# Feed-forward inputs on Trainium2: one product of 512 columns for high and low activations, and evacuation in two halves

## What is computed

```
D_MODEL = 1024; SEQ = 256; D_FF = 11 * D_MODEL // 4        # 2816
def _rmsnorm(x, g):
    y = x * lax.rsqrt(jnp.mean(x * x, axis=-1, keepdims=True) + 1e-6)
    return y * g
def _swiglu(h, w_in, w_out):
    a, b = jnp.split(h @ w_in, 2, axis=-1)
    return (jax.nn.silu(a) * b) @ w_out
x = x + 0.5 * _swiglu(_rmsnorm(x, g), w_in, w_out)          # four times
```

## Time and profile before

| | us |
|---|---|
| median of 3 runs (2226.9 to 2237.2) | 2232.5 |
| profiled execution, its own time | 2229.4 |
| its span | 2227.7 |
| TensorE (PE) matmuls busy | 2143.9 |
| weight loads (PEld) busy | 1878.6 |
| VectorE (DVE) busy | 1384.0 |
| ScalarE (ACT) busy | 847.6 |

### The profile page before, as it was taken

One profiled execution on the slowest core, in us unless ns is written; L12 is line 12 of the kernel. 1 busy time (PEld: TensorE's weight loads), 2 busy tenths in 40 slices (PEclk: granted clock), 3 DMA queues, 4 the chain that ended last, 5 costly groups with the idle time before them and its releaser, 6 DMA issues.

```text
span 2227.7 us, 43246 instructions
## 1 busy us (share of the span) xinstructions
PE 2143.9 (96%) x17274; PEld 1878.6 (84%) x17274; DVE 1384.0 (62%) x2303; ACT 847.6 (38%) x1336; POOL 28.9 (1%) x58
## 2 busy tenths in 40 slices
PE   7999999999999999899999999999999999999998
PEld 7999878999999998899986676788888876559987
DVE  6666657666666677766664556674355355657854
ACT  4444634444444444444531444421111233334332
POOL 0000000000000000000000000000000000000000
PEclk9999999999999999999999999999999999989999
DMA  7665424665666552466641110222222222003544
GB/s 269 245 228 185 167 75 175 241 238 183 240 237 224 198 182 99 167 229 246 226 176 38 39 39 20 102 76 94 94 95 94 95 95 95 1 19 120 182 174 147
DMA packets 50229, 325.73 MB, mean 146 GB/s; under 512 B 5328, under 2 KB 8656, under 8 KB 16976
## 3 DMA queue, kind: packets, MB, share of 16 engines
q1 hardware_dynamic: 42480, 266.62, 33.7%
q0 software_dynamic: 7648, 57.71, 6.9%
HBM read 323.26 MB, written 1.05 MB: 146 GB/s over the span
## 4 chain that ended last, share of the span: by engine, by line
PE 84%; DVE 9%; ACT 4%; issue 2%; DMA 0%; ACTq 0%; DVEq 0%; SPq 0%
PE psum L1914 17%; PE psum L1915 16%; PE psum L1916 16%; PE psum L2002 4%; PE psum L2003 4%; PE psum L2004 4%; PE psum L2499 3%; DVE w_lo L1062 2%; PE psum L2023 2%; PE psum L2338 2%; PE psum L2500 1%; ACT scratch L866 1%; ACT w_hi L620 1%; PE psum L2358 1%; PE psum L2321 1%
## 5 line engine op out<-in xcount | busy, mean ns | idle before, releaser
L1062 DVE TENSOR_TENSOR w_lo<-raw,w_hi 128x1024 fp32r<-128x1024 f32 (+1 forms) x534 | 590.2, 1146 | 229.3 <-ACT w_hi L620 215.3
L620 ACT ACTIVATE w_hi<-raw 128x1024 fp32r<-128x1024 f32 (+1 forms) x542 | 514.6, 991 | 572.3 <-PE psum L1916 351.6
L1914 PE MATMUL psum<-h_hi,w_hi 128*128 128x256 f32 (+1 forms) x2136 | 641.6, 300 | 12.8 <-DVE w_lo L1062 6.4
L1915 PE MATMUL psum<-h_lo,w_hi 128*128 128x256 f32 (+1 forms) x2136 | 633.5, 297 | 0.0
L1916 PE MATMUL psum<-h_hi,w_lo 128*128 128x256 f32 (+1 forms) x2136 | 633.1, 296 | 0.0
L1914 PEld LDWEIGHTS psum<-h_hi,w_hi 128*128 128x128 f32 x2136 | 410.1, 192 | 32.7 <-issue 12.8
L1916 PEld LDWEIGHTS psum<-h_hi,w_lo 128*128 128x128 f32 x2136 | 410.5, 192 | 10.1
L1915 PEld LDWEIGHTS psum<-h_lo,w_hi 128*128 128x128 f32 x2136 | 410.5, 192 | 9.8
L2002 PE MATMUL psum<-g_both,w_hi 128*128 128x256 f32 x704 | 202.2, 287 | 3.6 <-DVE w_lo L1062 3.6
L2003 PE MATMUL psum<-g_both,w_hi 128*128 128x256 f32 x704 | 199.3, 283 | 0.0
L2004 PE MATMUL psum<-g_both,w_lo 128*128 128x256 f32 x704 | 199.3, 283 | 0.0
(11 more groups left out here) (349 smaller groups left out, 3250.1 us busy)
## 6 DMA issues: line engine op xcount, KB each, us to landing
raw<-in_weights SPq DMA_DIRECT2D x207, 1024.0 KB, 4.8
raw_ada<-in_ada POOLq DMA_DIRECT2D x48, 1024.0 KB, 6.9
raw<-in_weights SPq DMA_DIRECT2D x64, 704.0 KB, 4.1
arena<-in_rpb POOLq DMA_DIRECT2D x1, 2048.0 KB, 10.9
arena<-in_fox_c POOLq DMA_DIRECT2D x1, 1696.0 KB, 9.2
const_region<-in_latent_c POOLq DMA_DIRECT2D x1, 1394.0 KB, 6.8
const_region<-in_even_c POOLq DMA_DIRECT2D x1, 1360.0 KB, 8.1
x_res<-in_x_lat SPq DMA_DIRECT2D x4, 256.0 KB, 7.1
```

The lines of the kernel that those rows point to most:

```text
L620: nc.scalar.activation(wh[s][:, a], raw[s][:, a], ACT.Copy).then_inc(hi_ready, 1)
L1062: V.tensor_tensor(wl[s][:, a], raw[s][:, a], wh[s][:, a].bitcast(F32), ALU.subtract).then_inc(lo_ready, 1)
L1914: mm(out, sh, mh, start=n == 0, stop=False)
L1915: mm(out, sh, ml, start=False, stop=False)
```

## The change

The activations' high and low parts become one tensor `h_both`. In the feed-forward input (TensorE, `wide_chunks` and `first_wide`), the two matmuls with `w_hi` become one of 512 columns over both parts, whose result takes a whole bank: columns 0 to 255 hold w_hi x high, 256 to 511 w_hi x low. The matmul with `w_lo` adds into columns 0 to 255. The gate half goes to bank 0 or 1 (3 in the first unit) and is signalled by its own semaphore `gate_done`; the value half goes to bank 4 or 5, signalled by `gemm_done`. To get a value, the two parts of a bank have to be added: ScalarE copies columns 256 to 511 to SBUF and VectorE adds them to columns 0 to 255. This happens for the gate half in the unit's own turn, and for the value half in the next turn, behind the conversion of the next panel; the bank is freed by the value half's sum.

```diff
-        hh = sb("h_hi", [P, DC, TJ], F32R)
-        hl = sb("h_lo", [P, DC, TJ], F32R)
+        h_both = sb("h_both", [P, 2, DC, TJ], F32R)
+        hh, hl = h_both[:, 0, :, :], h_both[:, 1, :, :]
...
             def swiglu(i, j):
...
+                if not first:
+                    up_copy(pos.e + 2 * i + j, 1 - j)
+                act.wait_ge(gate_done, n + 1)
+                nc.scalar.activation(ffn_gl, psum[:, FFN_FIRST if first else (pos.u + j) % 2, T:TJ],
+                                     ACT.Copy).then_inc(gate_low, 1)
+                if not first:
+                    g_high(n - 1, 2 * i + j - 1, 1 - j)
                 act.wait_ge(scaled_a, n + 1)
                 nc.scalar.activation(ffn_t[:, j, :], ffn_a[:, j, :], ACT.Tanh, scale=0.5).then_inc(tanh_done, 1)
-                act.wait_ge(bank_free, pos.u + 2 * i + j + 3)
-                nc.scalar.activation(flat(gh, (2 * i + j) * T, T), ffn_g[:, j, :], ACT.Copy).then_inc(g_hi_done, 1)
+
+            def up_copy(e, j, b=None):
+
+                act.wait_ge(gemm_done, e)
+                nc.scalar.activation(ffn_ul, psum[:, UP + ((pos.u + j) % 2 if b is None else b), T:TJ],
+                                     ACT.Copy).then_inc(up_low, 1)
+
+            def g_high(n, c, j):
+
+                act.wait_ge(ffn_made, n + 1)
+                nc.scalar.activation(flat(gh, c * T, T), ffn_g[:, j, :], ACT.Copy).then_inc(g_hi_done, 1)
...
                 stage(11, 2, 1, 2, swiglu, peel=1, lead=lead)
+                up_copy(pos.e, 1, (pos.u - 1) % 2)
+                g_high(pos.n("unit") + 21, 21, 1)
...
+                def up(n, j, u):
+
+                    dve.wait_ge(up_low, n + 1)
+                    V.tensor_tensor(e_tmp[:], psum[:, UP + u % 2, 0:T] if isinstance(u, int) else
+                                    psum[:, UP + (pos.u + j) % 2, 0:T], ffn_ul, ALU.add).then_inc(bank_free, 1)
+                    freed(u)
+                    dve.wait_ge(ffn_seq, n + 1)
+                    V.tensor_tensor(ffn_g[:, j, :], ffn_u[:], e_tmp[:], ALU.mult).then_inc(ffn_made, 1)
...
-                    dve.wait_ge(gemm_done, pos.e + 2 * i + j + 1)
-                    V.tensor_tensor(ffn_a[:, j, :], ps_a, n_inv, ALU.mult).then_inc(scaled_a, 1)
-                    if not (peeled and j == 0):
+                    else:
+                        up(n - 1, 1 - j, u - 1)
+                    dve.wait_ge(gate_low, n + 1)
+                    V.tensor_tensor(n_add, psum[:, FFN_FIRST if first else b, 0:T], ffn_gl, ALU.add).then_inc(gate_sum, 1)
+                    dve.wait_ge(gate_sum, n + 1)
+                    V.tensor_tensor(ffn_a[:, j, :], n_add, n_inv, ALU.mult).then_inc(scaled_a, 1)
+                    if not first:
                         low(n - 1, 1 - j, c - 1)
-                        freed(u - 1)
                     dve.wait_ge(tanh_done, n + 1)
...
-                    V.tensor_tensor(ffn_g[:, j, :], ffn_u[:], ps_b, ALU.mult).then_inc(bank_free, 1)
...
+            def wide_chunks(b, s):
+
+                for m, (o, done) in enumerate(((b, gate_done), (UP + b, gemm_done))):
+                    for k in range(DC):
+                        w_hi, w_lo = wtile(s, k, m, 2 * P)
+                        mm(psum[:, o, :], w_hi, h_both[:, :, k, 0:T], start=k == 0, stop=False)
+                        ins = mm(psum[:, o, 0:T], w_lo, hh[:, k, 0:T], start=False, stop=k == DC - 1)
+                    ins.then_inc(done, 1)
```

More of the change, by code:

```diff
@@ L240, in build @@
         ada_done = sem("ada_done")
+        gate_done, gate_low, gate_sum = sem("gate_done"), sem("gate_low"), sem("gate_sum")
+        up_low, ffn_made = sem("up_low"), sem("ffn_made")
         v_made, v_scaled = sem("v_made"), sem("v_scaled")
@@ L1109, in evac @@
                 def evac(i, j):
                     peeled = isinstance(i, int) and i == 0
+                    first = peeled and j == 0
                     u = pos.u + 2 * i + j
                     n, c = n0 + 2 * i + j, 2 * i + j
-                    bank = (pos.u + j) % 2
-                    ps_a, ps_b = psum[:, bank, 0:T], psum[:, bank, T:2 * T]
-                    if peeled and j == 0:
+                    b = (pos.u + j) % 2
+                    if first:
                         inverse_norm()
-                        ps_a, ps_b = psum[:, FIRST, 0:T], psum[:, FIRST + 1, 0:T]
@@ L1121, in evac @@
+                    V.tensor_tensor(ffn_a[:, j, :], n_add, n_inv, ALU.mult).then_inc(scaled_a, 1)
+                    if not first:
                         low(n - 1, 1 - j, c - 1)
-                        freed(u - 1)
                     dve.wait_ge(tanh_done, n + 1)
+                    if not first:
+                        dve.wait_ge(ffn_made, n)
                     V.scalar_tensor_tensor(ffn_u[:], ffn_t[:, j, :], 1.0, ffn_a[:, j, :], ALU.add,
                                            ALU.mult).then_inc(ffn_seq, 1)
-                    dve.wait_ge(ffn_seq, n + 1)
@@ L1134, in evac, with last @@
                         ada_add(ab + i)
-                return evac, lambda: low(n0 + 21, 1, 21)
+                def last():
+                    up(n0 + 21, 1, pos.u - 1)
+                    low(n0 + 21, 1, 21)
+                return evac, last
             def ada_turn(k):
@@ L1962, in first_chunks, with first_wide @@
                 return ins
+            def wide_chunks(b, s):
[5 more added lines that the diff above has]
+                    ins.then_inc(done, 1)
+            def first_wide(s):
+                for k in range(DC):
+                    if k == DC - 1:
+                        first_sum()
+                    pe.wait_ge(h_ready, pos.n("h", 1))
+                    for m, (o, done) in enumerate(((FFN_FIRST, gate_done), (UP + pos.u % 2, gemm_done))):
+                        w_hi, w_lo = wtile(s, k, m, 2 * P)
+                        mm(psum[:, o, :], w_hi, h_both[:, :, k, 0:T], start=k == 0, stop=False)
+                        ins = mm(psum[:, o, 0:T], w_lo, hh[:, k, 0:T], start=False, stop=k == DC - 1)
+                        if k == DC - 1:
+                            ins.then_inc(done, 1)
             def first_sum():
@@ L1981, in into @@
                     bank(pos.u + 2 * i + j)
[L1982 to L1983 removed]
+                    if isinstance(i, int) and i == 0 and j == 0:
+                        first_wide(s)
+                    else:
+                        wide_chunks((pos.u + j) % 2, s)
                     if j == 0:
```

9 lines of the change are left out of this document (4 added, 5 removed).

## The result

| | before | after |
|---|---|---|
| median, us | 2236.8 (10 runs, 2226.9 to 2239.6) | 2221.4 (10 runs, 2216.3 to 2230.0) |
| profiled execution, own time | 2229.4 | 2225.0 |
| its span | 2227.7 | 2223.3 |
| its granted clock, mean | 0.986 | 0.983 |

The ratio is 0.9936, with an interval of 0.9919 to 0.9953: faster, by 15.5 us between the medians, where 20.9 were forecast. The direction was right and the time lies inside the range, but the largest term of the forecast's sum, the price of a pair of products, came out at half its size. The kernel before has ten runs here and had three when the forecast was made; its median moved from 2232.5 to 2236.8 us, so 4.3 of the 9.8 us between forecast and measured time are no fault of the sum.

A forecast was written before the change was run, and what follows sets the result against it. TensorE's matmul stream in the feed-forward input was taken as the bound. Shorter pairs 17.1, starts 2.0 and ends 1.8 summed to 20.9 us, taken from 2232.5 to forecast 2211.6 us, range 2204 to 2222.

The forecast's parts named there:

- the price of a pair of products: Feed-forward input, TensorE: a group costs 0.3467 us in place of 0.36, worth 17.1 us over 1280 groups.
- What bounds the kernel: Feed-forward input: TensorE is busy 120 of 120 us, so only a shorter TensorE stream helps if other engines keep up.
- Neither bound of the range: Best case 2205.8 us with all edge stalls gone; worst 2219.5 with dearer sums and half a microsecond lost per edge.
- The prediction's own sign of being wrong: Input stage: a turn above 12.4 us, late TensorE stalls on value sum or low part, or pair spacing near 0.36.
- Rival 1: Input stage: separate blocks or switching output forms keep spacing at 0.36 us; only edges pay, 3.8 us, 2228.7; 6 in 100.
- The loop, 5.5 us: VectorE and ScalarE, conversion start to tanh end: 5.5 us against TensorE's 6.16 a unit, so it fits.
- Rival 2: Input units: the loop of VectorE and ScalarE becomes the bound at 6.6 us a unit, 2252 us in all; 4 in 100.
- The added waits at zero: Input units: the bank is free 3.8 us behind a unit's end, TensorE asks at 5.55 or 6.76; no wait added.
- "as before": Turns with a modulation panel: VectorE's transpose waits until about 1.1 us behind the unit's end, unchanged by the change.
- The starts, 0.5 us each: Start of each feed-forward: third unit 7.0 us behind the reciprocal in place of 7.49, 2.0 us over four.
- The ends, 0.45 us each: End of each feed-forward's input: conversion 0.45 us earlier in a stall of 0.94, 1.8 us over four.
- The sum: Whole kernel: 17.1 + 2.0 + 1.8 = 20.9 us gained, giving 2211.6 us.

The follow-up runs named there:

- the run with adjacent blocks: The changed kernel with high and low activations laid side by side chunk by chunk, blocks 2 KB apart in place of 16 KB: 2224.2 us, ratio 0.9962.
- the grouped kernel: The changed kernel with each half of a steady unit running its eight 512-column products first, then its eight of 256: 2217.1 us, ratio 0.9928.

## Why the prediction was wrong, and where it was right

- **What bounds the kernel: right.** TensorE stays busy throughout the window at clock 1.00, and only its stream counts.
- **"The trace holds that pair already ... 0.3467 us each ... 1280 groups x 0.0133 = 17.1 us": this step failed.** The pair does run at 0.3467, in the earlier trace rows and in some stretches after, but steady input turns run at 0.3533. What is saved is 0.36 - 0.3533 = 0.0067 us a group, 8.5 us, or by turns (12.74 - 12.53) x 40 = 8.4. One stretch of 256 pairs in one execution was taken as the price of the form. It was one of two prices, and another run has that very stretch at 0.3537. The gain was the difference of two near numbers, so that 2% more in one of them halved it. Neither bound of the range carried that; that the time lies in it, by 0.6 us, is luck: the room had been left for the edges, which came out near their forecast. The prediction's own sign of being wrong, a turn above 12.4 us, did come: 12.53. The Trainium skill, "TensorE: Matmul & The Clock Gate", "Back-to-back issue gap", gives the formula that the prediction quotes for an isolated matmul and not for a stream; its estimate of 325.0 ns lies further below this price than below the 0.3467.
- **Rival 1, the spacing stays at 0.36: half right.** Half of the saving came. Its first reason, two separate blocks, falls by the run with adjacent blocks. The second, switching between two output forms, has the grouped kernel for it, whose turns are all shorter; against it stand the stretches that alternate at 0.3467, as fast as if switching cost nothing. It stays open.
- **The loop, 5.5 us: right**, at 5.48. The assumed 0.45 for ScalarE's PSUM copy was 0.36 to 0.39. Rival 2 did not come, and the kernel with the value half in its own turn shows what it would have cost.
- **The added waits at zero: right.** No unit behind the third is stalled; the group of L2006 has 2.2 us of waiting for the value sum in all, 3 times. VectorE's transpose waited in the turns with a modulation panel, 39 times and 33.0 us in all; "as before" was wrong, since before it waited 3 times, 5.7 us. It cost TensorE nothing.
- **The starts, 0.5 us each: nearly.** The third unit starts 374.80 - 367.95 = 6.85 us behind the reciprocal, where 7.0 was forecast and 7.49 was before, and in three of the four the value sum releases it, as written. From the second unit's first product it is 0.60 to 0.65 us each, 2.5 in all, for a forecast of 2.0.
- **The ends, 0.45 us each: nearly.** The stall fell from 0.94 to 0.30 in the first; over the four the stretch from the first output product to the second panel's is 2.4 us shorter, for a forecast of 1.8.
- **The sum** with the measured price is 8.5 + 2.5 + 2.4 = 13.4 us, against 13.7 by the trace's stages (8.8 where 8.5 stands). The 15.5 between the medians is that and 1.8 more; the interval of the ratio reaches from 10 to 18 us and can't tell the two apart. 13.4 in place of 20.9 would have put the forecast at 2219.1.

## What to carry to other kernels

Where a gain is the small difference of two spacings, read the spacing in every stretch and every execution that holds the form, and let the range span them: a price from one stretch may be a state. Group products by width where the order is free, rather than alternating two widths; here that took another 0.12 us off each turn, in the one execution that was profiled. When a step's output comes in two parts, signal the first early and put the second's evacuation behind the next conversion, and look at the end of the stage for what the early signal earns: 7 us here, all of it there.

## What the runs showed of the hardware

A stream that alternates products of 512 and 256 columns, each with its own weight load, has two spacings at granted clock 1.00: 0.3467 and 0.3533 us a pair. It holds one for a stretch, up to 255 distances. In the faster (changed kernel, from 29.6 us) the next start comes 0.230 us behind a wide product and 0.117 behind a narrow one. In the slower (same trace, from 36.4 us) the distances repeat after three pairs: 0.240 and 0.120, 0.236 and 0.114, 0.232 and 0.118. So the difference sits behind the wide product.

The stride of the weights, the distance of the blocks, the order of banks and the activations' address don't select the spacing; with a stop or a spare product between stretches other stretches got the faster one. Long streams of one width settle at one spacing, 0.12 us at 256 columns and 0.2267 at 512, in every profiled execution, and their sum is the faster pair. A stream of 512 columns takes a few products to get there: in the kernel before, from 1455.6 us, after a first distance of 0.307 they are 0.235, 0.233, 0.236, 0.223, 0.231, 0.237, 0.227, 0.234 and 0.231, and then 0.226 to 0.227. The grouped kernel's halves show the same, with five such distances in each. What selects the spacing was not found, and it wasn't tried to alternate other widths.
